# The last expert turn of a two-layer decoder step cut into two turns of 896 columns

## The reference, cut to what matters

```python
def swiglu(h, wg, wu, wd):
    return (jax.nn.silu(h @ wg) * (h @ wu)) @ wd

def moe_swiglu(h, w_router, wg, wu, wd):
    logits = (h @ w_router).astype(F32)
    top_v, top_i = lax.top_k(logits, TOP_K)
    probs = jax.nn.softmax(top_v, axis=-1)
    comb = jnp.sum(jax.nn.one_hot(top_i, N_EXPERTS, dtype=F32) * probs[..., None], axis=-2)
    out = jnp.zeros_like(h)
    for e in range(N_EXPERTS):
        out = out + comb[..., e:e + 1] * swiglu(h, wg[e], wu[e], wd[e])
    return out
```

## Time and profile before

| | us |
|---|---|
| median of 3 runs | 1602.42 |
| lowest and highest of them | 1601.67, 1602.76 |
| the profiled execution's own time | 1603.74 |
| its span, from the first to the last instruction | 1602.1 |

### The profile page before, as it was taken

How to read it: one execution, slowest core, us unless ns; L and a number is a source line. 1 busy time by engine, 2 the same in 40 slices (tenths; PEclk the granted TensorE clock), 3 DMA queues, 4 the chain that set the end, 5 groups by cost and what they waited for, 6 DMA issues and landing times.

```text
span 1602.1 us, 37184 instructions
## 1 busy us (share of the span) xinstructions
PE 1564.8 (98%) x16734; PEld 987.4 (62%) x16734; DVE 541.4 (34%) x1182; ACT 181.5 (11%) x486; POOL 69.5 (4%) x118
## 2 busy tenths in 40 slices
PE   7999999999999999999999999999999999999987
PEld 3777898999997878944444444444444445555554
DVE  4368378666554784741001101110111011101132
ACT  2102303111112032131000000000000000000000
POOL 1112400000000110010000000000000000000010
PEclk9999999999999999999999999999999999999999
DMA  9999969666359745579999999999999999999995
GB/s 362 362 387 365 285 220 322 231 224 215 128 176 317 241 160 181 171 277 377 416 410 388 418 419 402 417 416 403 418 404 416 418 401 418 414 405 417 407 377 181
DMA packets 174339, 535.30 MB, mean 334 GB/s; under 512 B 12535, under 2 KB 101413, under 8 KB 161378
## 3 DMA queue, kind: packets, MB, share of 16 engines
q1 hardware_dynamic: 158274, 494.58, 80.8%
q0 software_dynamic: 8768, 28.96, 5.3%
q10 hardware_dynamic: 7136, 9.34, 1.8%
HBM read 517.47 MB, written 15.82 MB: 333 GB/s over the span
## 4 chain that ended last, share of the span: by engine, by line
PE 86%; DMA 9%; DVE 3%; issue 1%; ACT 1%; SPq 1%; ACTq 0%; DVEq 0%
PE banks L1890 33%; PE banks L1911 16%; PE banks L1204 14%; PE banks L1565 13%; DMA ring<-in_w_exp_up 5%; DMA ring<-in_w_in 2%; PE banks L1475 2%; PE banks L1745 2%; PE banks L1236 1%; DVE inv L2510 1%; PE banks L1732 1%; PE banks L1583 1%; DMA ring<-in_w_ada 1%; DMA ring<-in_w_exp_down 0%; PE banks L1614 0%
## 5 line engine op out<-in xcount | busy, mean ns | idle before, releaser
L1890 PE MATMUL banks<-ring,xT 128*32 128x448 f32 x3072 | 301.4, 539 | 2.9 <-DMA ring<-in_w_exp_up 2.9
L1890 PE MATMUL banks<-ring,area 128*32 128x448 f32 x3072 | 301.7, 539 | 1.3 <-DMA ring<-in_w_exp_up 0.8
L1565 PE MATMUL banks<-hT,ring 128*128 128x264 f32 x1024 | 238.0, 387 | 5.2 <-ACT hT L898 3.7
L577 DVE TENSOR_TENSOR area<-banks,area 128x448 f32<-128x448 f32 x48 | 45.7, 953 | 573.5 <-ACT area L1162 573.5
L1911 PE MATMUL banks<-area 128*32 128x256 f32 x3840 | 226.8, 379 | 1.7 <-issue 1.6
L1565 PEld LDWEIGHTS banks<-hT,ring 128*128 128x128 f32 x1024 | 191.9, 190 | 40.5 <-issue 8.6
L1890 PEld LDWEIGHTS banks<-ring,xT 128*32 128x32 f32 x3072 | 108.1, 110 | 163.7 <-issue 152.0
L1890 PEld LDWEIGHTS banks<-ring,area 128*32 128x32 f32 x3072 | 104.8, 110 | 167.4 <-issue 159.1
L1911 PEld LDWEIGHTS banks<-area 128*32 128x32 f32 x3840 | 132.8, 110 | 106.7 <-issue 45.3
L1162 ACT ACTIVATE area<-banks 128x448 f32<-128x448 f32 x48 | 26.1, 543 | 776.7 <-PE banks L1890 776.7
L1911 PE MATMUL banks<-ring,area 128*32 128x256 f32 x1536 | 89.2, 379 | 1.8 <-DMA ring<-in_w_exp_down 1.2
(11 more groups left out here) (362 smaller groups left out, 1255.2 us busy)
## 6 DMA issues: line engine op xcount, KB each, us to landing
ring<-in_w_exp_gate SPq DMA_DIRECT2D x128, 896.0 KB, 15.1
ring<-in_w_exp_up SPq DMA_DIRECT2D x128, 896.0 KB, 17.1
area<-in_w_exp_down SPq DMA_DIRECT2D x62, 1024.0 KB, 16.2
ring<-in_w_ada SPq DMA_DIRECT2D x96, 512.0 KB, 8.5
ring<-in_w_in SPq DMA_DIRECT2D x32, 1024.0 KB, 12.6
ring<-in_w_exp_down SPq DMA_DIRECT2D x32, 1024.0 KB
area<-in_w_exp_down SPq DMA_DIRECT2D x31, 512.0 KB
ring<-in_w_ff_gate SPq DMA_DIRECT2D x11, 1024.0 KB, 7.3
```

The lines of the kernel that those rows point to most:

```text
L577: dve.tensor_tensor(F["act_tok"][:, t, :].rearrange("p (i n) -> p n i", i=BODY), bank[3 + t][:, 0:SLICE].rearrange("p (n i) -> p n i", i=B ...
L1565: mm = pe.matmul(bank[b][:, 0:T], w[:, c, :], hT[:, c, :], start=(c == 0), stop=(c == DC - 1))
L1890: mm = pe.matmul(bank[t + 3 * half][32 * g:32 * g + 32, 0:SLICE], tokens[:, t, 32 * r:32 * r + 32], w[half][:, SLICE * g:SLICE * (g + 1)], ...
```

## The change

The last turn becomes two turns of half its width, m = 15 and m = 16 (`LAST` is 15, `TURNS` 17). Each has eight gate-up steps of 24 + 24 matmuls of 224 columns (they are 48 rows of the trace still) and seven down rows. Turn 15's pages, 128 x 896, lie in the first slot of each pair. Turn 16's pages lie in the second slots, which nothing else uses after turn 14. Turn 16's seven down rows are loaded into the first slots once turn 15 has used its pages. `LAST_ROWS` lays turn 14's 14 down rows between the steps 1 to 7 of turn 15, turn 15's seven rows behind the steps 1 to 7 of turn 16, and leaves turn 16's seven rows for the end. The diff, without the parts on ACT that only shorten the slices:

```diff
@@ -51,7 +51,26 @@
 SPANS = FE // P // SPAN
 SLICE = WIDE // 4
 TILES = CAP // 32
-TURNS = E * BODIES
+TURNS = E * BODIES + 1
+LAST = TURNS - 2
+ROWS = E * BODIES * BODY
+
+
+def turn_at(m):
+
+    if m < LAST:
+        return m // BODIES, m % BODIES, BODY
+    return E - 1, BODIES - 1 + m - LAST, BODY // 2
+
+
+def wide_of(m):
+    return turn_at(m)[2] * P
+
+
+def first_column(m):
+    return (BODIES - 1) * WIDE + (m - LAST) * WIDE // 2 if m >= LAST else m % BODIES * WIDE
+
+
 HALF = T // 2
 FF_CHUNKS = FF // P
 FF_PAIRS = FF_CHUNKS // 2
...
@@ -314,6 +333,9 @@
         DOWN_PAGES = ((0, 2), (2, 2), (4, 2), (6, 1), (7, 2), (9, 2), (11, 2), (13, 1))
         EARLY_ROWS = ((2, 2), (4, 2), (6, 1))
         DOWN_ROWS = ((0, 1), (2, 3), (4, 5), (6,), (7, 8), (9, 10), (11,), (12, 13))
+        LAST_ROWS = (((), (0, 1), (2, 3), (4, 5), (6, 7), (8, 9), (10, 11), (12, 13)),
+                     ((), (0,), (1,), (2,), (3,), (4,), (5,), (6,)),
+                     tuple((i,) for i in range(SPAN)) + ((),))
         PAIRED = ("z", "branch", "out", "gate", "up", "down")
         SUM_BANK = (1, 3, 2, 7)
         BIAS_BANK = (6, 7, 1, 5)
...
@@ -569,20 +591,21 @@
                 make_put()
                 dve.wait_ge(s.h_put, 16 * 6)
                 for m_ in range(TURNS):
-                    e, b = m_ // BODIES, m_ % BODIES
+                    e, b, body = turn_at(m_)
+                    n_cols = 32 * body
                     for t in range(TILES):
                         dve.wait_ge(s.silu_e, TILES * m_ + t + 1)
                         if m_:
                             dve.wait_ge(s.act_step, TILES * (m_ - 1) + t + 1)
-                        dve.tensor_tensor(F["act_tok"][:, t, :].rearrange("p (i n) -> p n i", i=BODY),
-                                          bank[3 + t][:, 0:SLICE].rearrange("p (n i) -> p n i", i=BODY),
-                                          F["silu_tok"][:, t, :].rearrange("p (n i) -> p n i", i=BODY),
+                        dve.tensor_tensor(F["act_tok"][:, t, 0:n_cols].rearrange("p (i n) -> p n i", i=body),
+                                          bank[3 + t][:, 0:n_cols].rearrange("p (n i) -> p n i", i=body),
+                                          F["silu_tok"][:, t, 0:n_cols].rearrange("p (n i) -> p n i", i=body),
                                           ALU.mult).then_inc(s.act_e, 1)
                     if m_ >= 2:
                         dve.wait_ge(s.d_used, BODY * (m_ - 1))
                     for t in range(TILES):
                         dve.wait_ge(s.act_e, TILES * m_ + t + 1)
-                        dve.transpose(F["actT"][:, m_ % 2, t, :], F["act_tok"][:, t, :]).then_inc(s.act_step, 1)
+                        dve.transpose(F["actT"][:, m_ % 2, t, 0:n_cols], F["act_tok"][:, t, 0:n_cols]).then_inc(s.act_step, 1)
                     if b == 0 and e < E - 1:
                         read_rows(e + 1)
                     if b == 0 and e == E - 1:
...
@@ -590,7 +613,7 @@
                         dve.wait_ge(s.gate_tok_out, 5)
                         for i in range(3):
                             add_picked(i)
-                dve.wait_ge(s.d_used, BODY * TURNS)
+                dve.wait_ge(s.d_used, ROWS)
                 gate = zeros[:, 0:S].unsqueeze(1)
                 dve.tensor_tensor(y_gated[:, 0:2, :], bank[6][:, :].rearrange("p (t n) -> p t n", t=2),
                                   gate.broadcast_to([P, 2, S]), ALU.mult).then_inc(s.y_gated, 1)
...
@@ -681,22 +704,30 @@
 
             def gate_up_pages(m, r):
 
-                e, b = m // BODIES, m % BODIES
+                e, c = turn_at(m)[0], first_column(m)
                 for half, w in ((0, A["w_exp_gate"]), (1, A["w_exp_up"])):
                     k = (2 * r + half) % DC
+                    at = eslot[2 * k + (m > LAST)]
                     if m == 0 and r < DC // 2:
                         sp.wait_ge(s.pages_used, STRAIGHT - RING + 2 * k + 2)
+                    elif m > LAST and r < DC // 2:
+                        sp.wait_ge(s.gu_used, DC * (LAST - 1) + r + DC // 2 + 1)
                     else:
                         sp.wait_ge(s.gu_used, DC * m + r - DC // 2 + 1)
-                    sp.dma_start(run(eslot[2 * k], 2)[:, 0:WIDE],
-                                 w[0, e, r * P:(r + 1) * P, b * WIDE:(b + 1) * WIDE]).then_inc(page_in[eslot[2 * k]], 16)
+                    pages = run(at, 2) if m < LAST else wide(at)
+                    sp.dma_start(pages[:, 0:wide_of(m)],
+                                 w[0, e, r * P:(r + 1) * P, c:c + wide_of(m)]).then_inc(page_in[at], 16)
 
             def down_rows_in(m, i, n):
 
-                e, b = m // BODIES, m % BODIES
-                rows = A["w_exp_down"][0, e, b * WIDE:(b + 1) * WIDE, :].rearrange("(p i) d -> p (i d)", i=BODY)
+                e, _, body = turn_at(m)
+                c = first_column(m)
+                rows = A["w_exp_down"][0, e, c:c + wide_of(m), :].rearrange("(p i) d -> p (i d)", i=body)
                 at = eslot[2 * DC + i % SPAN]
-                if m or i >= SPAN:
+                if m > LAST:
+                    at = eslot[2 * i]
+                    sp.wait_ge(s.gu_used, DC * LAST + DC // 2 + i // 2 + 1)
+                elif m or i >= SPAN:
                     sp.wait_ge(s.d_used, BODY * m + i - SPAN + n)
                 else:
                     sp.wait_ge(s.pages_used, STRAIGHT)
...
@@ -711,7 +742,11 @@
                     for r in range(DC):
                         if m < TURNS and (m or r >= DC // 2):
                             gate_up_pages(m, r)
-                        if m:
+                        if m > LAST + 1 and r < SPAN:
+                            down_rows_in(m - 1, r, 1)
+                        elif m == LAST + 1 and r < DC // 2:
+                            down_rows_in(m - 1, *DOWN_PAGES[r])
+                        elif m and m <= LAST:
                             i, n = DOWN_PAGES[r]
                             if m > 1 or (i, n) not in EARLY_ROWS:
                                 down_rows_in(m - 1, i, n)
...
@@ -1872,23 +1907,25 @@
 
             def gate_up_step(m, r):
 
-                e = m // BODIES
+                e, b, body = turn_at(m)
+                columns = body * 32
                 tokens = h_got[e % 2]
                 w = []
                 for half in range(2):
                     k = (2 * r + half) % DC
-                    at = eslot[2 * k]
-                    pe.wait_ge(page_in[at], landed[at] + 16 * (2 * m + (2 * r + half) // DC + 1))
-                    w.append(run(at, 2)[:, 0:WIDE])
+                    at = eslot[2 * k + (m > LAST)]
+                    turns = 2 * m if m <= LAST else 0
+                    pe.wait_ge(page_in[at], landed[at] + 16 * (turns + (2 * r + half) // DC + 1))
+                    w.append(run(at, 2) if m < LAST else wide(at))
                 for t in range(TILES):
                     if r == 0 and m:
                         pe.wait_ge(s.act_e, TILES * (m - 1) + t + 1)
-                    if r == 0 and m % BODIES == 0:
+                    if r == 0 and b == 0:
                         pe.wait_ge(s.h_got_out, TILES * e + t + 1)
                     for half in range(2):
                         for g in range(4):
-                            mm = pe.matmul(bank[t + 3 * half][32 * g:32 * g + 32, 0:SLICE], tokens[:, t, 32 * r:32 * r + 32],
-                                           w[half][:, SLICE * g:SLICE * (g + 1)],
+                            mm = pe.matmul(bank[t + 3 * half][32 * g:32 * g + 32, 0:columns], tokens[:, t, 32 * r:32 * r + 32],
+                                           w[half][:, columns * g:columns * (g + 1)],
                                            start=(r == 0), stop=(r == DC - 1), skip_group_check=True)
                     if r == DC - 1 and t < TILES - 1:
                         mm.then_inc(s.gu_mm, 1)
...
@@ -1904,13 +1941,16 @@
                     if b == 0 and e:
                         pe.wait_ge(s.y_read, 2 * e)
                 at = eslot[2 * DC + i % SPAN]
-                if i in [first for first, _ in DOWN_PAGES]:
+                if m > LAST:
+                    at = eslot[2 * i]
+                    pe.wait_ge(page_in[at], landed[at] + 16 * (2 * LAST + 3))
+                elif i in [first for first, _ in DOWN_PAGES]:
                     pe.wait_ge(page_in[at], landed[at] + 16 * (2 * m + i // SPAN + 1))
                 for t in range(TILES):
                     for q in range(4):
                         mm = pe.matmul(bank[6 + t // 2][32 * q:32 * q + 32, (t % 2) * S:(t % 2 + 1) * S],
                                        FFN["actT"][:, m % 2, t, 32 * i:32 * i + 32], wide(at)[:, q * S:(q + 1) * S],
-                                       start=(b == 0 and i == 0 and t != 1), stop=(b == BODIES - 1 and i == BODY - 1),
+                                       start=(b == 0 and i == 0 and t != 1), stop=(i == body - 1 and (m > LAST if e == E - 1 else b == BODIES - 1)),
```

(2 more changed lines are left out.)

6 lines of the change are left out of this document (3 added, 3 removed).

## The result

The changed kernel takes 1608.47 us (median of 5 runs, 1606.99 to 1611.42). The kernel before, run beside it, takes 1602.06 (5 runs, 1600.44 to 1602.76). The ratio is 1.0045, with an interval of 1.0031 to 1.006: 6.4 us slower by the medians, 7.2 by the ratio. The profiled execution took 1606.99 by its own time, the lowest of the five and 1.5 us under the median. That of before took 1603.74, 1.7 over its median.

What follows compares the result with a forecast made beforehand. PE, busy 98% of the span, was taken as the bound. 1560.9 - 5.4 (gathers earlier) + 0.6 + 37.1 (PE) + 2.0 (clock) + 12.2 (tail) = 1607.4 span, 1607.7 median; range 1604.0 to 1613.2.

Steps and rivals of the forecast that it cites:

- R3: Rival: pages and activations come early and PE never waits, 7.7 us less, 1594.7; chance 0.04.
- R1: Rival: the gathers on the DMA queues land no earlier, 10.7 us more, 1613.1; chance 0.15.
- R2: Rival: the gathers land 8 to 13 us earlier, result within 0.2% of no change; chance 0.12.
- R4: Rival: dearer narrow PE steps or half-size pages starving PE in turn 16, up to 2.6 us on top, 1610.3; chance 0.11.
- stores to POOL: ACT's stores, before POOL's gathers, end 2.0 us earlier beside smaller page packets.
- gathers: POOL's gathers of the rows DVE awaits take 3.4 us less beside smaller page packets.
- additions: DVE's twelve additions of the gathered rows, ahead of turn 15's products, take 15.39 us.
- wake-up and product: DVE's wake-up and one tile's product after the additions, before PE can go on: 0.6 us.
- PE from there on, with the clock: PE's turn 16 steps, 14 down rows and activation wait, 37.1 us, plus 2.0 for the clock's fall.
- The clock: PE's granted clock falls once after the stall and costs 2.0 us, bounds 0 and 3.5.
- The activation wait: PE waits 0.8 us for turn 16's activations before the last seven down rows.
- the length of the stall: PE ends turn 15 at 1545.1, then waits 9 to 16 us for DVE's product before turn 16's first step.

Runs made afterwards that it cites:

- The moved line: Changed kernel with DVE's twelve additions moved behind turn 15's transposes: 1603.4 us, ratio 1.0009; run again 1603.46 us, ratio 1.0008.
- the control: Kernel before the change with its twelve additions moved behind turn 15's transposes: 1602.03 us, ratio 1.0.
- the two further profiles: The changed kernel run again unaltered, on two more occasions: 1608.48 us, ratio 1.0038, and 1608.0 us, ratio 1.0051.
- half-page run: Kernel before the change with each gate and up page of turn 15 fetched by two DMAs of 896 columns: 1602.97 us, ratio 1.0004.
- the one with dummies: Changed kernel with 48 dummy matmuls on PE before turn 16's first step: 1605.97 us, ratio 1.0023.

## Why the prediction was right

**The mechanism** was the one forecast: additions in front of the products on DVE, one PE wait that a product ends, no gap on DVE between the two, and a clock at 0.51 afterwards. The moved line shows the cause, and the control shows that the same move changes nothing in the kernel before. R3 (faster) fell with this: the rows landed at 1538.36 and would have had to land by 1529.1, or by 1534.5 with turn 15 ending on PE where it really did, at 1550.53. R1 fell too, since they were earlier, and R2, whose 8 to 13 us they missed at 7.1, since the median is 6.4 us up. R4 had no effect to show: steps take 2.27 us in turn 16, and no page was late there.

**The sum, by its terms.** Predicted 1607.4 as a span, measured 1605.3, and 1606.3 and 1606.8 in the two further profiles. The table has the terms of the first. The median was forecast at 1607.7 and is 1608.47. That it is so near is in part luck: the sum starts from an execution of the kernel before that lay 1.7 us over the median of its five runs here, and the difference of the medians is 6.4 us where I had 5.3.

| term | predicted | measured |
|---|---|---|
| stores to POOL | -2.0 | -3.6 |
| gathers | -3.4 | -3.4 |
| additions | 15.39 | 15.39 |
| wake-up and product | 0.6 | 0.73 |
| PE from there on, with the clock | 39.1 | 38.87 |
| tail | 12.2 | 11.9 |

*The stores* were mis-sized. I priced them with one packet time of 174 ns for queue 1, said to be in proportion to its bytes. It isn't: the 6561 B a packet of the earlier trace rows (3.74 MB in 570) and 5120 B in my mix give 197 ns. Nor is there one price. In the kernel after, queue 1's packets take 153 ns during the stores (635 packets, share 86.5% from 1513 to 1520) and 198 during the gathers (573, 59.0% from 1524 to 1536). So the stores' term came out too small. For the gathers my own sum with 197 in place of 174 would have given 2.3 us and not 3.4; that the kernel after has 3.4 is luck. The half-page run gives 3.4 for the stores and 4.5 for the gathers. Counted from the stores to the rows' arrival, the gain is 7.9 us in that run and 6.9 in the kernel after, but 4.7 and 6.2 in the two further profiles of the changed kernel, 5.1 in the run with two additions moved and 6.2 in the one with dummies. The forecast of 5.4 lies among these. The mechanism (queues that take turns by the packet) holds for the gathers, with 573 packets against 579, and less strictly for the stores, with 635 against 448. The size of the gain varies from run to run by more than its distance from the forecast in the kernel after.

*The clock* cost 1.6 us (6.14 less 4.54), not 2.0; 1.4 and 2.4 in the other two profiles. The Trainium skill (TensorE: Matmul & The Clock Gate, "Why this matters for your kernels") warns of idle gaps between bursts of matmuls. The 0.51 agrees, and so does the run with dummies: with the gap filled the clock stays at 1.00, and the kernel is 2.5 us faster.

*The activation wait* was 0.59, not 0.8; Silu took 0.36 and the transposes 0.97.

**The step that failed** is the length of the stall. I expected 9 to 16 us, and it was 3.95, with 7.41 and 4.86 in the other profiles. I let PE end turn 15 at 1545.1, with no loss in the turn. The turn took 41.9 us in place of 36.3. In PE's timeline three idle times of 0.33 to 0.83 us are put down to issue, with four or five matmuls in 1.43 us between them. The kernel before has the same slow stretch, which the rows of the forecast don't show:

```profile
1530.98 0.64 PE L1911 MATMUL banks<-area 128*32 128x256 f32 x4 [0.81 <-issue]
```

The waits that I named (1.93, 0.58, 0.59 and 1.20) are 4.3 of the 8.6 us, and for the other half, the slowed work, I put nothing into the changed kernel's turn 15. In the kernel before the stretch alone is 2.7 us (two rows from 1527.56 to 1532.89, 5.3 us in place of 2.59). The error cost the sum nothing, because PE then waits for DVE anyway, as the forecast said of R4's losses. But it hid a real cost. I wrote that the 8.6 us could be won, and that the waits for late pages vanish. The runs without gathers show that some 40% of them go with the gathers, and that the split turn wins none that can be measured.

**What stays open.** Why PE slows during the gathers is not settled. Ten profiles have the slow stretch, of both kernels. The four that don't were all taken on one chip, and two of them have the gathers, so the runs without gathers don't show that the gathers make it. But in all ten the last of its gaps ends 1.3 to 1.5 us after POOL has issued its last gather (kernel after: 1527.20 and 1528.73, before: 1530.93 and 1532.41). It also moves with the gathers in the half-page run, where POOL starts 2.3 us earlier and the last gap ends 2.4 us earlier, at 1530.02. The gathers' bytes go on moving until 1538.36 in the kernel after, at a DMA share near 1, while PE is back at its full rate. So where the stretch comes, it keeps time with POOL's issuing of the gathers and not with the moving of their bytes. This is a coincidence in ten profiles and not an experiment; why PE slows, and why it doesn't in two profiles with gathers, no run shows.

The gathers' cost to the kernel is another matter. It is near what their bytes need: 528 rows of 4096 B are 2.16 MB, which take 5.2 us at the 413 GB/s of the windows. With the pages requested earlier, at a DMA share of 1.0 from 1520 to 1550, a wait taken away in turn 16 came back in turn 15. That this explains the 3.7 and 5.1 us is argued, not shown. Nor is it settled which part of the run-to-run spread (1606.99 to 1611.42) is clock. Runs near 1611.3 had a mean clock of 0.994, the profiled one 0.997.

## What to carry to other kernels

When a turn is shortened or split, look at the engine that works in a fixed written order, and ask what stands ahead of the hand-over that now comes earlier. Here 15 us of additions, hidden with 3.5 us to spare, came in front of it, and one moved line gave back 5 us. And test with the shared load taken away whether the waits that a change is to win can be won at all: in the split kernel, with DMA at its full rate, they only moved.

## What the runs showed of the hardware

Smaller packets in one queue speed up a small queue beside it. With the pages' rows halved from 7168 to 3584 B, the stores beside them went from 13.8 to 10.4 us and the gathers from 21.7 to 17.2, and the kernel's time stayed (ratio 1.0004). While the gathers move in the kernel after, from 1524 to 1536, its queues show (packets, MB, share):

```profile
q1 hardware_dynamic: 573, 2.73, 59.0%
q0 software_dynamic: 579, 1.99, 42.2%
```

The two queues move as many packets as each other, as they did before with larger pages. Queue 1 moves more only while the gathers' queue has little to move: 270 to 36 from 1521 to 1524, and 206 to 25 from 1536 to 1538.4. Beside the stores the counts are not equal: 635 to 448 from 1513 to 1520.

The granted clock fell after 3.95 us of idle time for 3.4 us (1554.4 to 1557.8), and after 7.41 us for some 4.8, an estimate from the mean of 0.65 over 6.9 us. It did not fall where 48 dummy matmuls bridged the gap (1.00 from 1555.8 to 1558.0).

PE can run at a fraction of its rate with nothing to wait for in the trace: 1.43 us for each four to five matmuls at full granted clock (0.83, 0.81 and 0.33 us "issue" between them in the kernel after). It begins 2 to 5 us after POOL's first gather and ends 1.3 to 1.5 us after the last one is issued, in ten of the twelve profiles with gathers.
